# GpSimd adds terms ahead of TensorE's sums over the partitions in the second block

## What is computed

```python
def second_block(x, mem, positions, ...):
    u = rms_norm_2(h, norm_mix_g[l])             # h is the first block's output, itself rms-normed: sum 1 (1024 terms)
    proj = u @ w_in[l]
    conv_in, c_q, c_kv, k_rope_raw, gate_logits = jnp.split(proj, cut, axis=-1)
    # mla_attention: rms_norm_2(c_q, ..)  sum 2 (384 terms);  rms_norm_2(c_kv, ..)  sum 3 (256 terms)
    # conformer_conv: glu, 31 taps, then layer_norm over 512 channels
    mu = jnp.mean(xf, axis=-1, keepdims=True)                      # sum 4
    var = jnp.mean(jnp.square(xf - mu), axis=-1, keepdims=True)    # sum 5
    y = (xf - mu) * lax.rsqrt(var + EPS)
```

## Time and profile before

| what | value |
|---|---|
| time, median of 3 runs | 2579.42 us (2579.03 to 2579.81) |
| the profiled execution's span | 2577.6 us |
| TensorE busy | 2559.2 us, 99% of the span |
| VectorE busy | 1450.2 us, 56% |
| ScalarE busy | 947.2 us, 37% |
| GpSimd busy | 384.2 us, 15% |

### The profile page before, as it was taken

The page is one execution under the profiler, slowest core; times in us unless marked ns, Lnnn a source line. Parts: engine busy times, 40 slices in busy tenths (PEclk is TensorE's granted clock), DMA queues, the critical chain, the costliest instruction groups (busy, mean ns, idle before and its releaser), DMA issues.

```text
span 2577.6 us, 32166 instructions
## 1 busy us (share of the span) xinstructions
PE 2559.2 (99%) x11610; PEld 2120.0 (82%) x11610; DVE 1450.2 (56%) x1735; ACT 947.2 (37%) x1381; POOL 384.2 (15%) x310
## 2 busy tenths in 40 slices
PE   8999999999999999999999999999999999999999
PEld 7888888888888888888888888888888888788887
DVE  7444347764443454443576644434999787642443
ACT  5222234432222232222354322223477534441332
POOL 4000111320001100001123100012177221100001
PEclk9999999999999999999999999999999999999999
DMA  5333332233333333333323333334233333233332
GB/s 160 98 98 94 97 87 83 82 100 96 98 96 96 102 91 97 98 92 98 96 66 91 98 97 98 94 96 126 73 81 76 123 90 112 76 107 97 98 98 82
DMA packets 487838, 247.21 MB, mean 96 GB/s; under 512 B 39874, under 2 KB 484551, under 8 KB 487495
## 3 DMA queue, kind: packets, MB, share of 16 engines
q1 hardware_dynamic: 487298, 245.75, 33.3%
q10 hardware_dynamic: 452, 0.32, 0.1%
HBM read 241.84 MB, written 4.19 MB: 95 GB/s over the span
## 4 chain that ended last, share of the span: by engine, by line
PE 95%; DVE 3%; ACT 1%; issue 0%; DMA 0%; POOL 0%; DVEq 0%; ACTq 0%
PE bank L669 15%; PE bank L668 15%; PE bank L670 15%; PE psT L668 10%; PE psT L669 10%; PE psT L670 10%; PE psS L668 4%; PE psS L669 4%; PE psS L670 4%; PE bank L684 1%; PE bank L677 1%; PE bank L680 0%; PE psT L778 0%; DVE wlo L1755 0%; PE bank L1083 0%; PE bank L1082 0%
## 5 line engine op out<-in xcount | busy, mean ns | idle before, releaser
L1755 DVE TENSOR_TENSOR wlo<-raw,whi 128x1024 fp32r<-128x1024 f32 x466 | 626.3, 1345 | 434.0 <-ACT whi L1285 417.4
L668 PE MATMUL bank<-xhi,whi 128*128 128x512 f32 x1656 | 648.1, 391 | 1.4 <-issue 1.4
L669 PE MATMUL bank<-xlo,whi 128*128 128x512 f32 x1656 | 644.7, 389 | 0.0
L670 PE MATMUL bank<-xhi,wlo 128*128 128x512 f32 x1656 | 644.6, 389 | 0.0
L1285 ACT ACTIVATE whi<-raw 128x1024 fp32r<-128x1024 f32 x463 | 485.3, 1050 | 340.5 <-PE psT L670 316.9
L668 PEld LDWEIGHTS bank<-xhi,whi 128*128 128x128 f32 x1656 | 311.0, 188 | 67.1 <-issue 2.9
L669 PEld LDWEIGHTS bank<-xlo,whi 128*128 128x128 f32 x1656 | 311.0, 188 | 64.7 <-issue 1.4
L670 PEld LDWEIGHTS bank<-xhi,wlo 128*128 128x128 f32 x1656 | 310.8, 188 | 64.9
L668 PE MATMUL psT<-hhi,whi 128*128 128x512 f32 x704 | 273.9, 389 | 0.0
L669 PE MATMUL psT<-hlo,whi 128*128 128x512 f32 x704 | 273.9, 389 | 0.0
L670 PE MATMUL psT<-hhi,wlo 128*128 128x512 f32 x704 | 273.9, 389 | 0.0
(11 more groups left out here) (516 smaller groups left out, 3457.5 us busy)
## 6 DMA issues: line engine op xcount, KB each, us to landing
raw<-in_ffn_wg SPq DMA_DIRECT2D x88, 512.0 KB
raw<-in_ffn_wu SPq DMA_DIRECT2D x88, 512.0 KB
raw<-in_ffn_wd SPq DMA_DIRECT2D x64, 512.0 KB
raw<-in_w_mlp SPq DMA_DIRECT2D x64, 512.0 KB
raw<-in_w_in SPq DMA_DIRECT2D x53, 512.0 KB
raw<-in_ffn_wd SPq DMA_DIRECT2D x32, 384.0 KB
raw<-in_w_in SPq DMA_DIRECT2D x24, 256.0 KB
raw<-in_w_out SPq DMA_DIRECT2D x11, 512.0 KB
```

The source lines that it names most:

```text
L668: pe.matmul(dest, a, rhs_hi(k), start=start and k == 0, stop=False)
L669: pe.matmul(dest, a, rhs_lo(k), start=False, stop=False)
L670: mm = pe.matmul(dest, b_, rhs_hi(k), start=False, stop=stop and k == tiles - 1)
L1755: dve.tensor_tensor(wlo[:, a:a + UNIT], raw[:, a:a + UNIT], whi[:, a:a + UNIT].bitcast(F32), ALU.subtract).then_inc(s_split, 1)
```

## The change

Seven of the fifteen matmuls by ones go. In their place GpSimd adds chunks together, and TensorE waits for GpSimd's semaphore `s_xn`:

- sum 1: GpSimd adds VectorE's rest (chunk 4) to its own; one matmul instead of two.
- sum 2: GpSimd adds `lsq` 0 to 1; two matmuls instead of three.
- sum 3: GpSimd adds `lsq` 3 to 4; one instead of two.
- sum 4: GpSimd adds `zc` 0 and 1 into `var`, between two of its tap additions of slot 5; three instead of four.
- sum 5: GpSimd adds the four squares in three additions, at the end of its slot 13; one instead of four, and it stands one step later in slot 14's unit (k == 3).

```diff
@@ TensorE
             in_unit("q", 1)
-            pe.wait_ge(s_xn, 3)
-            pe.matmul(psS[:, 0:S], ones[:, :], chunk(sq7, 0), start=True, stop=False)
-            pe.wait_ge(s_v7, 6)
-            pe.matmul(psS[:, 0:S], ones[:, :], chunk(sq7, 4), start=False, stop=True).then_inc(s_ss, 1)
+            pe.wait_ge(s_xn, 4)
+            pe.matmul(psS[:, 0:S], ones[:, :], chunk(sq7, 0), start=True, stop=True).then_inc(s_ss, 1)
...
             pe.wait_ge(s_lq, QC)
-            ones_sum(psS[:, 0:S], [chunk(lsq, m) for m in range(QC)]).then_inc(s_ss, 1)
+            pe.wait_ge(s_xn, 5)
+            ones_sum(psS[:, 0:S], [chunk(lsq, m) for m in range(1, QC)]).then_inc(s_ss, 1)
...
-            pe.wait_ge(s_lq, QC + KVC)
-            ones_sum(psS[:, 512:1024], [chunk(lsq, QC + m) for m in range(KVC)]).then_inc(s_ss, 1)
+            pe.wait_ge(s_xn, 6)
+            ones_sum(psS[:, 512:1024], [chunk(lsq, QC + KVC - 1)]).then_inc(s_ss, 1)
...
             def conv_square_sums():
-                for j, a in enumerate(ln_sq):
-                    pe.wait_ge(s_lsq, j + 1)
-                    mm = pe.matmul(tap_b, ones[:, :], a[:, :], start=j == 0, stop=j == CC - 1)
-                mm.then_inc(s_ss, 1)
+                pe.wait_ge(s_xn, 10)
+                pe.matmul(tap_b, ones[:, :], ln_sq[0][:, :], start=True, stop=True).then_inc(s_ss, 1)
...
-                in_unit(*FILL[s], ready=(lambda k: conv_square_sums() if k == 2 else None) if s == LN_VAR + 1 else None)
+                in_unit(*FILL[s], ready=(lambda k: conv_square_sums() if k == 3 else None) if s == LN_VAR + 1 else None)
...
-                    ones_sum(tap_b, [chunk(zc, i) for i in range(CC)]).then_inc(s_lsum, 1)
+                    pe.wait_ge(s_xn, 7)
+                    ones_sum(tap_b, [var[:, :], chunk(zc, 2), chunk(zc, 3)]).then_inc(s_lsum, 1)
@@ GpSimd
+            pool.wait_ge(s_xn, 3)
+            pool.wait_ge(s_v7, 6)
+            pool.tensor_tensor(chunk(sq7, 0), chunk(sq7, 0), chunk(sq7, 4), ALU.add).then_inc(s_xn, 1)
+            for j in (1, QC + KVC - 1):
+                pool.wait_ge(s_lq, j + 1)
+                pool.tensor_tensor(chunk(lsq, j), chunk(lsq, j), chunk(lsq, j - 1), ALU.add).then_inc(s_xn, 1)
...
+                    if a + 1 == len(POOL_TAPS) // 2 + 2:
+                        pool.wait_ge(s_tap, TAPS)
+                        pool.wait_ge(s_pa, len(POOL_TAPS) // 2)
+                        pool.tensor_tensor(var[:, :], chunk(zc, 0), chunk(zc, 1), ALU.add).then_inc(s_xn, 1)
...
+                if s == LN_VAR:
+                    for n, (j, k) in enumerate(((0, 1), (2, 3), (0, 2))):
+                        pool.wait_ge(s_lsq, max(j, k) + 1)
+                        if n == 2:
+                            pool.wait_ge(s_xn, 9)
+                        pool.tensor_tensor(ln_sq[j][:, :], ln_sq[j][:, :], ln_sq[k][:, :], ALU.add).then_inc(s_xn, 1)
```

More of the change, by code:

```diff
@@ L327, in build @@
         h_q = sem("head_q_projected")
-        s_xn = sem("squares7_added")
+        s_xn = sem("terms_of_sums_added")
         s_ro = sem("rope_step")
```

## The result

The changed kernel takes 2585.81 us (median of 8 executions, 2582.99 to 2587.30), the kernel before 2578.96 in the same session. The ratio is 1.0024, with a 95% interval of 1.0015 to 1.0032: slower by 6.85 us. The executions before lie within 1.3 us of each other; those of the changed kernel spread over 4.3 us, and their mean granted clock goes with it: 0.997 in the five from 2585.7 up, 0.998 or 0.999 in the three from 2583.0 to 2584.0. The profiled one is among the faster: 2583.39, span 2581.6.

The account below looks back on a forecast made before the run. TensorE was taken to bound the kernel (95% of the chain that ended last). +0.05 (places 1 to 3), 2.1 (places 4 and 5) and 1.5 (clock) gave +3.65 on the 2579.42 median: 2583.1 us, range 2580.4 to 2586.0.

Parts of the forecast that it names:

- fourth rival: Clearly slower: clock stays low longer than at the start; with 8 us low, 6.2 us lost, 2585.6; chance 0.16.
- Most of the chance, 0.79: Chance given to "same", within about 0.2% (5.2 us) of no change; slower had 0.18, faster 0.03.
- Places 1 to 3: Sums 1 to 3: net -0.25, -0.8 and +1.05 us, together +0.05 (bounds -0.8 and +1.5).
- VectorE's 0.7 us: At sum 2: VectorE had waited 0.69 us for this sum, so its chain comes forward by about that, no more.
- a saving at sum 1 or 3: Listed among the trace findings that would show the prediction wrong; no size given.
- Place 4: Sum 4: slot 5's addition delays GpSimd's list 1.43 us, taken up by 1.95 us idle; cost 0, at most 0.3.
- Sum 4's saving: At sum 4: the sum ends 0.86 us sooner; TensorE is that far ahead, no other engine is.
- Place 5: Sum 5: three additions take 4.3 us, TensorE stands still 5.5 us and ends 2.1 late, sums saved included.
- The clock's term: Clock falls in sum 5's pause; 3 us at low clock, costing 1.5 us (between 0.5 and 2.5).
- Sum 3's stall: At sum 3: TensorE waits 1.9 us for GpSimd's addition and saves 0.86, net +1.05.
- the 2.9 us at the program's end: At the program's end: 2.9 us of standing still brought the clock to 1.2 GHz; sum 5's longer 5.5 us pause should too.
- the clock holds: First rival: only one fall is seen, at the program's end, so clock holds; 2.2 us, 2581.6; chance 0.24.

Follow-up runs that it names:

- e9: The kernel before with sum 3 alone changed (one matmul over the two added squares instead of two): 2579.93 us, +1.04, ratio 1.0004.
- e4: The kernel before with sums 1 and 2 alone changed: 2578.68 us, -0.35, ratio 0.9998.
- e3: The kernel before with sum 4 alone changed, GpSimd's addition between two tap additions of slot 5: 2580.04 us, +1.01, ratio 1.0004.
- e7: The kernel before with sum 4 alone changed, its addition behind GpSimd's last tap in slot 12 instead of in slot 5: 2578.96 us, -0.05, ratio 1.0.
- e2: The changed kernel with sum 5 as before: 2580.48 us, +1.45 against the kernel before, ratio 1.0007.
- e10: The changed kernel with 20 overwritten matmuls ahead of sum 5 and 8 ahead of sum 3: 2581.96 us, ratio 1.0012 against the kernel before.
- e5: The changed kernel with 20 matmuls ahead of sum 5 whose result the sum overwrites: 2583.37 us, ratio 1.0015 against the kernel before.
- e8: The changed kernel with sum 5's three additions ahead of the scaling of slot 13's probabilities: 2583.16 us, ratio 1.0016 against the kernel before.
- e6: The changed kernel with sum 5 at step 7 of slot 14's unit instead of step 3: 2583.40 us, ratio 1.0016 against the kernel before.
- e12: The kernel before with sums 1 and 2 changed, sum 4's addition in slot 12, one early addition at sum 5: 2579.22 us, +0.33, ratio 1.0.
- e1: The kernel before with sum 5 alone changed (one matmul, three additions by GpSimd): 2582.23 us, +3.20, ratio 1.0013.

## Why the prediction was right in kind and short in size

The forecast was 2583.1 in a range of 2580.4 to 2586.0; 2585.81 lies in the range, at its upper end. As a change it was +3.65 and came out +6.85, since the kernel before took 2578.96 here and not 2579.42. That the median still lies in the range is in part luck: two of the eight executions are above it, and its upper end leans on the fourth rival's 8 us of low clock in one stall, which no trace shows. The profiled execution, 2583.39, is near the forecast, but it is one of the faster three, and errors cancel in it. Most of the chance, 0.79, stood on less than 5.2 us (0.2%). The kernel is slower without doubt; whether by more than 0.2% is not decided, as the interval, 0.15% to 0.32%, has that bound inside.

**Places 1 to 3: right, a little small.** +0.34 us against +0.05. The waits are 0.24 (0.6 foreseen), none for GpSimd at sum 2, and 1.96 (1.9). They come to 0.3 us less than foreseen, and the cost to 0.3 more: at each of the three sums TensorE loses 0.2 to 0.3 us beyond its wait less the 0.86 (e9 has the same at sum 3). The sum had no such term, and what it is, the runs don't show. That only VectorE's 0.7 us would come forward by sum 2 fits e4, which keeps 0.6 to the end. The prediction's sign of being wrong, "a saving at sum 1 or 3", contradicts its own -0.25 at sum 1; measured there is -0.36.

**Place 4: a cost put at nothing.** "0, at most 0.3" for the shift of GpSimd's list. It costs 0.93 us in the trace and 1.01 alone (e3), and with the addition elsewhere nothing (e7). The step looked only for who waits for GpSimd, found 1.95 us of room and stopped. It left out the other direction of the lock that it had itself used a paragraph earlier: a shifted GpSimd holds off other instructions of VectorE, 1.1 us each for two of them, and VectorE does not catch that up before slot 8.

**Sum 4's saving: right.** TensorE is 0.87 us ahead behind it. It is swallowed, in the changed kernel at sum 5's stall, in e3 and e7 in slot 16.

**Place 5: the stall right, the clock mis-sized.** TensorE's wait is 4.94 us (5.5 foreseen), three additions take 3.89 us (4.3), each at the free price. Without the clock the place costs 4.76 - 2.06 = 2.70 us, swallowed lead included, against 2.1 + 0.86 = 2.96. VectorE's L1758 is 4.0 us later than before; the sum itself takes 2.08 us at the low clock in place of 1.12 at the full one, and without that it is 3.0 (2.8 foreseen). The clock's term was 3 us low for 1.5. In the profiled execution it is low over 4.6 us of matmuls for 2.1, of which slot 16 gives 0.6 back (below). So in this trace the forecast's 1.5 is met; at the median it is 3.8. In most executions the low clock must last longer: the mean clock of 0.997 against 0.998 says so, though no trace shows one of them. The fourth rival (2585.6) had the right result and only half of the reason: it wanted 8 us of low clock in this one stall.

**A fall of the clock that was not foreseen.** Sum 3's stall was priced as 1.9 us of time and nothing else. The prediction held only the 5.5 us pause against the 2.9 us at the program's end; a pause shorter than 2.9 was not asked about. In a part of the executions the clock falls there too and it costs 1.7 us more (e2). The two together are worth 3.8 us at the median, where 1.5 had been set down. The rival "the clock holds", +2.2 us, gets its test in e10: +3.07, the difference being place 4's 0.93. That its 2581.6 is so near to e10's 2581.96 is chance.

**Slot 16: given back.** 0.65 us of the delay vanish from sum 5 to slot 17 in steps of 0.1 to 0.3: short waits of TensorE for VectorE that the late TensorE no longer meets. Before, its weight loads waited 0.23 and 0.19 us for VectorE's `pt2l` (L2218) in slots 16 and 17; after, not at all. In e5, where the clock holds, these waits are still there (0.17 and 0.23) and only 0.07 us vanish: a low clock delays TensorE and not the chain, and then the chain's waits cover a part of it. From sum 1 to the end e5's trace pays 3.0 us and the changed kernel's 4.5, so the clock costs 1.5 net. The forecast had no such term.

In sum, for the profiled execution: 3.65 + 0.29 (places 1 to 3) + 0.93 (place 4) - 0.26 (sum 5) + 0.56 (clock) - 0.65 (slot 16) = 4.52 us, measured 4.51. To the median come about 2.3 us, 6.85 in all. They are the clock's too: without its falls the kernel is at +3.07 (e10, median), with this trace's fall at 4.5.

**What stays open.** Which executions suffer, and what exactly brings the clock down. At sum 3 it held through 1.47 us in all eleven executions of e9. Through 1.93 to 1.96 us it held in three traces (the changed kernel, e5, e8), and it fell in two (e2, e6), 0.2 and 1.3 us after TensorE had gone back to work. In slot 16 it fell behind waits of 1.41 (e6) and 1.27 us (e12). The length of the wait alone does not decide it. Whether the low stretches in the slower executions of the changed kernel lie at sum 5, at sum 3 or in slot 16 was not seen, for want of a trace of one.

## What to carry to other kernels

Work taken from the bounding engine is worth its time only if what that engine waits for next also comes sooner; here 0.86 us at sum 4 was worth zero, because what TensorE waits for next hangs on other engines, and the seven savings together cost 6.85 us. Before an addition goes to GpSimd, look at both sides of its port: which VectorE instructions stand beside it and beside everything that it pushes back, not only at who waits for GpSimd. And a stall of TensorE is to be priced with the clock behind it, as a spread over executions: if harmless matmuls in the stall make the kernel faster and its times even, it was the clock.

## What the runs showed of the hardware

- After a pause of about 2 us of a TensorE that is otherwise fully busy, its clock falls to 1.2 GHz in some executions and not in others: behind the same wait at sum 3 it fell in the traces of e2 and e6 and held in those of e5, e8 and the changed kernel. The price is 1.7 us (e2), and 1.4 in slot 16 of e12. That makes a kernel's times scatter by 4.3 us where they had lain within 1.3. The Trainium skill (TensorE: Matmul & The Clock Gate, What's actually happening) says that the chip's watch on activity runs free of the kernel, and that the slow stretch at a kernel's start varies from run to run for that reason; the two groups of e1, e2 and e5 fit it, here in the middle of a kernel.
- Twenty-eight extra matmuls, 6.8 us of TensorE's time, made the changed kernel 3.8 us faster at the median (e10).
- GpSimd's addition of 128x512 in fp32 takes 1.26 to 1.29 us free, 1.5 to 2.3 beside VectorE, and lengthens VectorE's instruction by about 1.1 us (0.69 to 1.78, 1.23 to 2.31).
